# The squares of the input norm stored token by token: a sum that reads in order and a square that writes with a stride

## The reference

```python
def _rmsnorm(x, g):
    y = x * lax.rsqrt(jnp.mean(x * x, axis=-1, keepdims=True) + RMS_EPS)
    return y * g

for i in range(DEPTH):                                   # DEPTH = 4
    h = h + 0.5 * _rmsnorm(_swiglu(_rmsnorm(h, g[0, 0]), ffn_w_in[i, 0], ffn_w_out[i, 0]), g[0, 1])
    u = _rmsnorm(h, g[1, 0])
    m = mixer(u)           # i mod 3: 0 stick-breaking, 1 multi-head latent attention, 2 RWKV-7
    h = h + _rmsnorm(m, g[1, 1])
    h = h + 0.5 * _rmsnorm(_swiglu(_rmsnorm(h, g[2, 0]), ffn_w_in[i, 1], ffn_w_out[i, 1]), g[2, 1])
return h[:, N_META:]
```

## Time and profile before

| what | us |
|---|---|
| median of three runs | 2764.04 (2759.89 to 2766.44) |
| the profiled execution's own time | 2766.6 |
| its span, first to last instruction | 2764.8 |
| TensorE busy in the span | 2515.3 (91%) |
| DVE busy | 1653.8 (60%) |
| ACT busy | 1040.1 (38%) |
| POOL busy | 1841.0 (67%) |
| mean granted TensorE clock, share of full speed | 0.932 |

### The profile page before, as it was taken

The page is one execution under the profiler, slowest core; times in us unless marked ns, Lnnn a source line. Parts: engine busy times, 40 slices in busy tenths (PEclk is TensorE's granted clock), DMA queues, the critical chain, the costliest instruction groups (busy, mean ns, idle before and its releaser), DMA issues.

```text
span 2764.8 us, 51378 instructions
## 1 busy us (share of the span) xinstructions
PE 2515.3 (91%) x19334; PEld 2429.5 (88%) x19334; DVE 1653.8 (60%) x2064; ACT 1040.1 (38%) x1478; POOL 1841.0 (67%) x885
## 2 busy tenths in 40 slices
PE   7998989989987899999968788888899899898997
PEld 7998889989987899999958788876799899898997
DVE  7843368558633489289285844445687487315882
ACT  4443443433433443343445311112444334334342
POOL 6887368868864378877878722222688688773786
PEclk9999999999988999999968888786899999999999
DMA  5554235535533145535523300000255355451453
GB/s 186 170 198 130 92 114 175 197 118 171 197 107 97 61 137 184 173 129 174 176 72 114 100 1 1 1 1 1 94 173 195 117 174 188 138 168 62 159 178 118
DMA packets 89413, 348.39 MB, mean 126 GB/s; under 512 B 9952, under 2 KB 11104, under 8 KB 89184
## 3 DMA queue, kind: packets, MB, share of 16 engines
q1 hardware_dynamic: 89312, 347.01, 38.1%
HBM read 345.93 MB, written 1.05 MB: 125 GB/s over the span
## 4 chain that ended last, share of the span: by engine, by line
PE 73%; DVE 15%; ACT 4%; issue 4%; POOL 3%; DMA 0%; DVEq 0%; ACTq 0%; SPq 0%; POOLq 0%
PE bank L304 19%; PE bank L306 19%; PE bank L305 19%; PE bank L692 4%; PE bank L682 2%; DVE m L1316 2%; POOL w_lo L1149 1%; DVE acc L1275 1%; DVE hid_hi L1340 1%; DVE x_lo L1268 1%; DVE hid L1338 1%; DVE rstd L1261 1%; ACT w_hi L790 1%; POOL h L1162 1%; POOL x_lo L1175 1%
## 5 line engine op out<-in xcount | busy, mean ns | idle before, releaser
L1149 POOL TENSOR_TENSOR w_lo<-raw,w_hi 128x1024 fp32r<-128x1024 f32 (+2 forms) x608 | 1605.9, 2667 | 585.1 <-ACT w_hi L790 585.0
L304 PE MATMUL bank<-x_hi,w_hi 128*128 128x272 f32 (+1 forms) x3412 | 1002.8, 294 | 37.9 <-POOL x_lo L1175 14.8
L306 PE MATMUL bank<-x_hi,w_lo 128*128 128x272 f32 (+1 forms) x3412 | 992.8, 291 | 0.0
L305 PE MATMUL bank<-x_lo,w_hi 128*128 128x272 f32 (+1 forms) x3412 | 989.3, 290 | 0.0
L790 ACT ACTIVATE w_hi<-raw 128x1024 fp32r<-128x1024 f32 (+2 forms) x608 | 660.3, 1115 | 230.0 <-PE bank L306 212.6
L304 PEld LDWEIGHTS bank<-x_hi,w_hi 128*128 128x128 f32 x3412 | 651.0, 191 | 51.7 <-issue 35.3
L305 PEld LDWEIGHTS bank<-x_lo,w_hi 128*128 128x128 f32 x3412 | 652.9, 191 | 0.3
L306 PEld LDWEIGHTS bank<-x_hi,w_lo 128*128 128x128 f32 x3412 | 651.8, 191 | 0.0
L1342 DVE TENSOR_TENSOR hid_lo<-hid,hid_hi 128x272 f32 (+3 forms) x176 | 416.4, 2366 | 20.2
L304 PE MATMUL bank<-hid_hi,w_hi 128*128 128x272 f32 (+1 forms) x1408 | 404.9, 288 | 1.1 <-POOL w_lo L1149 1.0
L306 PE MATMUL bank<-hid_hi,w_lo 128*128 128x272 f32 (+1 forms) x1408 | 405.1, 288 | 0.0
(11 more groups left out here) (277 smaller groups left out, 2882.4 us busy)
## 6 DMA issues: line engine op xcount, KB each, us to landing
raw<-in_ffn_in SPq DMA_DIRECT2D x352, 512.0 KB, 3.2
raw<-in_ffn_out SPq DMA_DIRECT2D x128, 704.0 KB, 4.1
raw<-in_sb_in SPq DMA_DIRECT2D x48, 512.0 KB, 3.2
raw<-in_rw_in SPq DMA_DIRECT2D x24, 512.0 KB, 3.6
raw<-in_sb_out SPq DMA_DIRECT2D x16, 512.0 KB, 3.2
raw<-in_mla_out SPq DMA_DIRECT2D x8, 512.0 KB, 3.6
raw<-in_rw_lora SPq DMA_DIRECT2D x8, 512.0 KB, 4.3
raw<-in_rw_out SPq DMA_DIRECT2D x8, 512.0 KB, 3.5
```

The source lines that it names most:

```text
L304: nc.tensor.matmul(o, wh, xh[:, k, cols()], start=start, stop=False)
L305: nc.tensor.matmul(o, wh, xl[:, k, cols()], start=False, stop=False)
L306: last = nc.tensor.matmul(o, wl, xh[:, k, cols()], start=False, stop=stop)
L1149: nc.gpsimd.tensor_tensor(w_lo[:, s, w], raw[:, s, w], w_hi[:, s, w], ALU.subtract).then_inc(lo_ready, 1)
```

## The change

A second view of `m`'s bytes is made, `squares_by_token`, in which a token's eight tiles are neighbours: element (token l, tile t) lies at 8 l + t. The square still reads `h` tile by tile and in order, and writes each tile's 272 squares at a step of 8 elements, 32 bytes. The reduce reads the eight squares of token after token, in order, and writes `acc` as before. Counts of elements and instructions, engines, waits and their order stay. With 256 tokens left both use tokens 16 to 271 of the view.

```diff
@@ build @@
+        squares_by_token = m[:, :, :].rearrange("p t l -> p (t l)").rearrange("p (l t) -> p l t", t=DT_)
@@ gained, on ACT @@
-                nc.scalar.activation(m[:, :, cols()], h[:, :, cols()], ACT.Square).then_inc(hsq_ready, 1)
+                nc.scalar.activation(squares_by_token[:, cols(), :].rearrange("p l t -> p t l"), h[:, :, cols()], ACT.Square).then_inc(hsq_ready, 1)
@@ input_norm, on DVE @@
-                nc.vector.tensor_reduce(acc[:, cols()], m[:, :, cols()].rearrange("p t l -> p l t"), AX.X, ALU.add).then_inc(hacc_ready, 1)
+                nc.vector.tensor_reduce(acc[:, cols()], squares_by_token[:, cols(), :], AX.X, ALU.add).then_inc(hacc_ready, 1)
```

## The result

The changed kernel took 2775.97 us (median of four runs, 2771.96 to 2779.27) against 2761.97 us for the kernel before beside it. The ratio is 1.0042, 95% interval 1.0030 to 1.0055: slower by 8 to 15 us. The forecast was 2747 us, faster.

A forecast was written before the change was run, and what follows sets the result against it. TensorE, 73% of the chain, waits 20.1 us for the string of square, reduce and sum in the norms. Reduce 14.7 plus clock 2.7 gives 17.4 us off 2766.6, so 2749.2, or 2746.6 for the median (forecast 2747); range 2741 to 2771.

The forecast's parts named there:

- The square: ACT's square ahead of the reduce: strided writes add nothing to 2005 ns; bounds nothing and 2.2 us added.
- A write can be left behind: Ground for a free square: an engine must have a read before going on, but can leave a write behind.
- Its step is 34 times longer: Ground for a free square: the priced strided read, the reduce's, has a step 34 times longer than the write's.
- Rival B: Square's write pays what the reduce's read saves, 1.53 us a norm: 2763 us, or 2765 at 1.8 us; chance 0.27.
- D: Square's write at the reduce's pace or worse, 2.2 us added, more clock falls: 2769 to 2776, value 2775; chance 0.15.
- The reduce: DVE's reduce, read in order, falls from 3956 ns to 2.425 us; all norms together save 14.7 us of TensorE's waiting.
- Rival C: Reduce's 3956 ns go into closing 272 sums of eight, not the order: 2764 us with a free write; chance 0.08.
- The first norm: First norm, where the reduce waits for DVE's earlier work: gives its 1.08 us, and the square has 4.4 us to spare.
- The latent norm: The latent attention's norm, where the sum has no idle time ahead of it: gives nothing.
- two copies that have 5 us to spare: Work after the norm: a longer square would delay only two copies, which have 5 us to spare.
- What comes after: After the sum: TensorE reaches the freed bank 0.9 us after it is free, so the wait doesn't move there.
- The clock: TensorE's clock fell after four of ten waits, losing 5.5 us; half, 2.7 us, taken as regained, bounds 0 and 5.5.

The follow-up runs named there:

- experiment 5: Changed kernel with the stride moved to ACT's read: the square reads h token by token and writes in order; 1.0030 of the kernel before.
- experiments 3 and 4: Changed kernel with two (3) or four (4) tiles side by side, write step 8 or 16 bytes; 0.9937 and 1.0024 of the kernel before.
- Experiment 1: Changed kernel with the square's edit undone, so only the reduce's read is changed; 0.9937 of the kernel before.
- Experiment 6: Changed kernel with the sum matmul placed 18 matmuls later (HSUM_AT 5 for 2); 1.0014 of the kernel before.
- experiment 2: Changed kernel with the reduce's edit undone, so only the square's write is changed; 1.0127 of the kernel before.

## Why the prediction was wrong

**The square** is the step that failed: "I take nothing added." It was 2.41 us, from 2005 to 4417 ns (L839), in nine norms ahead of the reduce on the string, and TensorE's wait grew by 7.5 us where 14.7 less were summed. Both grounds given for nothing were wrong. "A write can be left behind" fails against experiment 5: a strided write costs ACT as much as a strided read, and a little more (4117 and 4417 ns for 4022). "Its step is 34 times longer" fails against experiments 3 and 4: the price follows whether two elements share 16 bytes (2178 and 4117 ns), and little the length of the step beyond that (4417 at 32 bytes). The upper bound was too low as well, 2.2 us added, because it took the read's pace for the worst. The row at hand, the reduce at 1.82 ns an element, was the best guide to the write, at 1.92, and was put aside.

The Trainium skill's rule that every access to a new line of 16 bytes pays (SBUF — State Buffer, Door 1: The DMA port swizzle), weighed in the prediction, had the write right in kind, as 4417 for 2005 ns shows, and would have given a time near no change. Rival B stood for it with 0.7 to 0.83 ns added for each element; measured were 2412 / 2176 = 1.11 ns.

**The rival that came out** is D: its place (L839 on the string in nine norms), its price (2.2 us or more; 2.41), its point of decision and its value, 2775 us, all fit. It had a chance of 0.15, and the range ended at 2771, short of the median by 5 us. That the value fits to 1 us is luck in part, for two terms were off and offset each other. D had 6.0 less 1.1 us of waiting, and the waits grew by 7.5: in the nine norms the square took 4.45 us, not the group's mean of 4.42 or D's 4.2. It had up to 7 us of clock for five more falls, and in the profile there were two more, 3.0 us. And it started from a median of 2764, where the kernel before took 2762 beside the changed one.

**The reduce** was right to 6 ns: 2.425 us forecast, 2.419 measured, and 2290 against 2286 for 256 tokens. Rival C, the closing of the sums, is dead. Experiment 1 alone would have been the forecast: 14.7 us summed and 14.6 found in the waits. That the 17.4 with the clock met the 17 in time is partly luck, since all four falls went and not half of them.

**The first norm** gave its 1.08 us, as said. **The latent norm** was not free: "two copies that have 5 us to spare" did not hold there. From the square's start to the sum it was 6.50 us before (808.84 to 815.34) and is 6.87 now (812.96 to 819.83), 0.4 us more. The two copies, the high parts of the next weights, now start only at 816.99 us, behind the square, and the low part made from the first ends at 819.8, right ahead of the sum.

**What comes after** held: no new wait at a bank or a low half took up the change. Experiment 6 made the bank's wait show, 9.1 us in ten norms, 0.9 each where 1.4 was expected, so the 4.0 us from the reduce's end to the freed bank hold to half a microsecond.

**The clock** was right in kind (no falls behind waits of 1.2 us or less). The four falls were taken at 5.5 us; by the missing matmuls they are 6.2 (49 x 0.126), since the prediction's windows ended before the clock was back. It is a term to carry: in experiment 2 it made a third of the loss, and no wait shows it.

## What to carry to other kernels

A change of layout has two sides, and both must be priced where they lie: when the maker and the reader of a buffer follow each other on the same string, moving the stride from one to the other wins nothing. Here each element that opened a 16-byte line of its own cost 1.7 to 1.9 ns on either side, and two neighbours sufficed, so the half-way layout took the whole gain. Before tuning the pace of an instruction at the end of a string, see what of it could start earlier: the square cut by tile gained as much as the faster reduce, and pairs squared two by two gained more than either. A wait that a view lists is not yet time: experiment 6 took 10 us off the waits and won about what the clock gave back.

## What the runs showed of the hardware

Float32 elements at a step of 8 bytes cost ACT's write 0.17 us over 2176 elements in order, at 16 bytes 2.1 us, at 32 bytes 2.4 us. A read of pairs is as fast on DVE as one of eight neighbours (2419 ns both), and a read at 1088 bytes costs ACT and DVE nearly the same (4022 and 3956 ns). TensorE's standstills of 1.9 to 2.3 us (the kernel before) were followed by a lower clock some of the time (4 of 9), of 2.9 to 3.3 us (the changed kernel) in 6 of 9, of 4.3 to 4.7 us (experiment 2) always (9 of 9), of 1.2 us or less never in these profiles, and matmuls that nobody needed kept the clock up. A fall of 3.4 us cost 12 matmuls, 1.5 us. Matmuls beside them slowed the strided instructions by 2%, the reduce at 1088 bytes from 3956 to 4036 ns and the square at 32 bytes from 4417 to 4500, and left those in order as they were (2419 and 2007 ns). Where TensorE stood still for 4.5 us (experiment 2), the strided reduce took 3866 ns.
